# Expert stage: indices, gates and destinations read in place, and the first four experts' weights loaded one stage earlier

## The chip, the cores and the metric

The kernel runs on one core of one Trainium2 chip. The metric is the device time of a whole execution in microseconds (us), the median of several runs. A second source is one profiled execution, in which the hardware profiler records each instruction and each DMA transfer. Engine names are those of the profile: PE is the matrix engine (TensorE), PEld its weight load, DVE is VectorE, ACT is ScalarE, POOL is GpSimd and SP is SyncE, which here only issues transfers (SPq is its queue of instructions).

## The reference

One layer of a streaming encoder: attention and an RWKV-7 recurrence from one projection, a LayerNorm, then a mixture of experts with two levels of routing, and a second LayerNorm. The part that matters here is the mixture of experts:

```
def hier_moe(h, moe_w):                      # h: 2048 + 32 tokens x 1024
    grp  = argmax(h @ w_gr + b_gr)           # one of 4 groups
    e_in = (h @ w_er + b_er)[grp]            # 8 experts of that group
    top_p, top_i = top_k(softmax(e_in), 2)   # two experts for each token
    gate = top_p / sum(top_p) * p_grp
    ...                                      # assignments sorted by expert, in blocks of rows
    def run_block(xb, e):
        return (silu(xb @ w_eg[e]) * (xb @ w_eu[e])) @ w_ed[e]
    y = zeros.at[token].add(run_block(...) * gate)
```

There are 32 experts, each with three matrices of 1024 x 256 (or 256 x 1024) floats, 1024 KB each. All data is float32.

## The kernel before

The program is a sequence of stages, each a block in which every engine runs its own list of instructions, with a barrier between two stages: mixer, attention, router, dispatch, experts, combine. All loops are written out, so the order on each engine is fixed when the program is built.

**Dispatch** (from line 1903) sorts the assignments. It fills 64 blocks of 128 rows (`NBLK`); each expert's rows begin at a new block, and the blocks left over at the end repeat the last expert with rows that go to a spare place. It leaves three tables in SBUF: `kept_tokens` (the output row of every block row, an integer), the gates in the first 64 columns of `kept_onehot`, and in the next 256 columns the row numbers that the gathers use, as floats (lines 2062 to 2069). SP does nothing in this stage.

**Experts** (from line 2072) runs over the 64 blocks, two to a turn, with two copies (s = 0 and 1) of every buffer. For one block:

- POOL gathers the block's 128 rows of `scr_hx` with four indirect DMAs (line 2153) into `ex_x`; the row numbers are first copied to a small buffer `ex_idx` (line 2149).
- DVE transposes them in four pieces to `ex_xT` (line 2321).
- PE multiplies by the gate and the up matrix (line 2252, 16 matmul records each), ACT takes the tanh (2200), DVE makes `ex_hid` (2328, 2332), PE transposes that (2267), ACT copies it to `ex_hT` (2205), PE multiplies by the down matrix (2276, 8 records).
- ACT writes `ex_y` from `ex_down`, scaled by the row's gate, in two halves (line 2212). The gate column is a copy that POOL made in `ex_gcol` (line 2160).
- POOL adds `ex_y` into `scr_acc` in HBM with one indirect DMA that accumulates (line 2171); the row numbers are a copy in `ex_dest` (line 2168). Two additions may not be under way at once, since two blocks can name the same row, so each waits for the one before it to have landed.

Within a turn i POOL's order is: both gate copies, the eight gathers of turn i + 2, then the addition of block 0, then that of block 1 (`turn`, line 2174). ACT's order is fixed too: for each block the tanh, the copy to `ex_hT` of the block before, and the result of the block before. ACT does not wait for the landed addition itself before it writes `ex_y` again; it waits for POOL's marks `gate0` and `dest0` (line 2210), which stand behind such a wait on POOL.

The weights lie in four slots (`SLOTS`). SP loads expert e into slot e mod 4 when expert e - 4 has left it (line 2127) and when expert e - 2 has landed (line 2124), so at most two loads are under way. PE may start an expert when `ready` says that its weights are there.

The lines quoted in the prediction are in the functions below.

Of the kernel before, what the change touches and what calls it, by code (L numbers as in the profile page):

```python
# [142 lines left out]
    ).split(),  # L143
    "gather_gpsimd": (
        "idx0 idx1 "
    ).split(),
    "add_gpsimd": (
        "gate0 gate1 dest0 dest1 "
# [193 lines left out]
def first_of_router(nc):  # L342
# [5 lines left out]
    return t  # L348

# [1286 lines left out]
def router(nc, io, scr, keep):  # L1636
# [6 lines left out]
    with ExitStack() as ctx:  # L1643
# [12 lines left out]
        ahead = scr["first_of_dispatch"] = Placed(nc, given.start - 4 * (3 * P + 96 + 56), cst=[3, P], nums=[96], cols=[56])  # L1656
# [246 lines left out]
def dispatch(nc, io, scr, keep):  # L1903
# [3 lines left out]
    with ExitStack() as ctx:  # L1907
# [12 lines left out]
        given = scr["first_of_dispatch"]  # L1920
        cst, nums = given.tiles["cst"], given.tiles["nums"][:, 0:KB + NBLK]
# [35 lines left out]
        block = ctx.enter_context(nc.Block())  # L1957

# [113 lines left out]
def experts(nc, io, scr, keep):  # L2072
# [4 lines left out]
    with ExitStack() as ctx:  # L2077
        def sb(name, shape, dt=F32):
# [6 lines left out]
        nought = sb("nought", [P, 1])  # L2085
        spare = [sb(f"spare{s}", [P, 1]) for s in range(2)]
        spare_y = [sb(f"spare_y{s}", [P, 1]) for s in range(2)]
        dest = [sb(f"dest{s}", [P, 1], I32) for s in range(2)]
        gcol = [sb(f"gcol{s}", [P, 1]) for s in range(2)]
        started = ctx.enter_context(nc.semaphore("ex_started"))  # L2090
        wg, wu, wd = sb("wg", [P, SLOTS, KC * FE]), sb("wu", [P, SLOTS, KC * FE]), sb("wd", [P, SLOTS, FC * D])

        idx, x, xT, th, hid, hT, y = ([sb(f"{n}{s}", shape, dt) for s in range(2)] for n, shape, dt in (
            ("idx", [P, 4], I32), ("x", [P, 4, FE], F32), ("xT", [P, KC, P], F32), ("th", [P, FE], F32),
# [6 lines left out]
        apol, bpol = Steps(nc, ctx, "gather_gpsimd"), Steps(nc, ctx, "add_gpsimd")  # L2101
        w_in = [Dmas(nc, ctx, f"ex_w_in{s}", 3, 1) for s in range(SLOTS)]
# [7 lines left out]
        def _(sp):  # L2110
            sp.dma_start(ident[:], io["ident"]).then_inc(const.sem, 16)
            for s in range(SLOTS):
                sp.sem_inc(w_in[s].sem, 16 * 3)

            def turn(t):
# [6 lines left out]
                for s, e in enumerate(es):  # L2122
# [4 lines left out]
                    sp.wait_ge(down.sem, free_at[s])  # L2127
                    for dst, src in ((wg, io["w_eg"]), (wu, io["w_eu"])):
                        w_in[s].go(sp.dma_start(dst[:, s, :], src[e].rearrange("a (p k) n -> (a p) (k n)", k=KC)))
# [6 lines left out]

        @block.gpsimd
        def _(g):
            g.memset(nought[:], 0.0).then_inc(started, 1)
            g.wait_ge(started, 1)  # L2140

            for own in (apol, bpol):
                g.sem_inc(own.sem, own.per)
# [474 lines left out]
```

## Time and profile before

| | us |
|---|---|
| median of 3 runs | 3268.62 (3267.7 to 3272.02) |
| the profiled execution, whole | 3262.0 |
| its span (first to last instruction) | 3259.1 |
| PE busy (matmul) | 2919.8 (90%) |
| DVE, ACT, POOL busy | 1740.4, 967.0, 587.6 |
| DMA engines, mean | 95 GB/s, 310.23 MB |
| mean granted PE clock | 0.954 |

The times in the rows below are microseconds from the start of the span, so that stages can be placed: dispatch begins at 2416, experts at 2452.7, combine at 3201.5. "Idle before" is the time an engine stood still before an instruction, with what ended it.

### The profile page before, as it was taken

The page shows a single profiled execution, that of the slowest core. Times are in us where ns is not written, and L with a number is a line of the kernel's source. Part 1 is how long each engine was busy: PE and PEld are TensorE (multiplying, and loading weights), DVE is VectorE, ACT ScalarE, POOL GpSimd, SP SyncE. Part 2 cuts the span into 40 slices and gives each one's busy share as a digit, 9 for nine tenths or more (in the row PEclk, how much of TensorE's full clock was granted, in tenths as well). Part 3 has the DMA queues.
Part 4 walks back from the last instruction along what each step waited for, and adds up shares of the span by engine and source line. Part 5 has one row for each costly group of instructions (what it writes and reads, how often), then busy time and mean ns, then how long its engine had stood idle before and what let it go on. Part 6 is the DMA issues. An engine that isn't in the chain of part 4 may idle for free. (4 is left out here: it accounts for less than half of the span.)

```text
span 3259.1 us, 66235 instructions
## 1 busy us (share of the span) xinstructions
PE 2919.8 (90%) x26600; PEld 2220.4 (68%) x26600; DVE 1740.4 (53%) x3820; ACT 967.0 (30%) x2497; POOL 587.6 (18%) x875
## 2 busy tenths in 40 slices
PE   7999999999999999669898998899957999989990
PEld 6888888888888888545555555555535776666770
DVE  1666666666666666558686868622253222222225
ACT  2333333333333333234443444312211111111115
POOL 0001000000000000010000000011104645555650
PEclk9999999999999999689999999999968999999995
DMA  6111121211111112420101010034318899776546
GB/s 192 35 38 36 37 40 37 39 37 36 37 37 36 38 37 40 93 86 1 38 1 39 1 35 1 34 117 129 129 52 304 257 371 291 241 228 164 104 95 245
DMA packets 337227, 310.23 MB, mean 95 GB/s; under 512 B 235201, under 2 KB 290529, under 8 KB 322529
## 3 DMA queue, kind: packets, MB, share of 16 engines
q1 hardware_dynamic: 315424, 238.88, 24.1%
q0 software_dynamic: 21504, 67.13, 9.2%
q8 instruction: 217, 3.56, 0.5%
q14 instruction: 82, 0.66, 0.1%
HBM read 208.12 MB, written 84.42 MB: 90 GB/s over the span
## 5 line engine op out<-in xcount | busy, mean ns | idle before, releaser
L802 PE MATMUL mx_bank<-mx_xT,mx_w_in 128*128 128x128 f32 x5168 | 647.6, 282 | 17.3 <-DVEq L286 13.8
L802 PEld LDWEIGHTS mx_bank<-mx_xT,mx_w_in 128*128 128x128 f32 x5168 | 606.3, 195 | 83.3 <-issue 60.6
L1485 PE MATMUL at_bank<-pl_kT,pl_qT 128*128 128x512 f32 (+5 forms) x656 | 291.1, 530 | 2.3 <-issue 2.3
L1457 ACT ACTIVATE at_PQ<-at_bank,at_nms 128x512 f32<-128x512 f32 (+5 forms) x328 | 192.7, 596 | 253.6 <-DVE at_nms L1585 252.1
L2276 PE MATMUL ex_down<-ex_wd,ex_hT 128*128 x512 | 236.4, 605 | 26.9 <-ACT ex_hT L2205 25.4
L2153 POOL DMA_INDIRECT ex_x<-scr_hx,ex_idx x256 | 247.0, 965 | 68.1 <-issue 60.1
L2252 PE MATMUL ex_gate<-ex_wg,ex_xT 128*128 x1024 | 234.1, 382 | 17.5 <-SPq L2125 17.5
L2252 PEld LDWEIGHTS ex_gate<-ex_wg,ex_xT 128*128 128x128 f32 x1024 | 196.3, 192 | 71.3 <-issue 47.3
L2212 ACT ACTIVATE ex_y<-ex_down,ex_gcol 128x512 f32<-128x512 f32 x128 | 81.0, 683 | 525.4 <-POOL ex_gcol L2160 186.1
L2252 PE MATMUL ex_up<-ex_wu,ex_xT 128*128 x1024 | 231.6, 379 | 0.0
L1628 DVE COPY at_PT<-at_bank 128x512 f32<-128x512 f32 (+3 forms) x328 | 196.3, 600 | 45.7 <-PE at_bank L1497 28.0
L1516 PEld LDWEIGHTS at_bank<-at_PT,at_vals 128*64 128x64 f32 (+1 forms) x2208 | 118.0, 137 | 150.4 <-issue 78.1
L2321 DVE STREAM_TRANSPOSE ex_xT<-ex_x 128x256 f32<-128x256 f32 x256 | 141.0, 608 | 145.3 <-DMA ex_x<-scr_hx,ex_idx 145.3
L1497 PE MATMUL at_bank<-pl_at_ident,at_PQ 128*128 128x128 f32 x1104 | 186.0, 284 | 22.9 <-ACT at_PQ L1457 12.8
L2252 PEld LDWEIGHTS ex_up<-ex_wu,ex_xT 128*128 128x128 f32 x1024 | 190.3, 191 | 23.2
L1497 PEld LDWEIGHTS at_bank<-pl_at_ident,at_PQ 128*128 128x128 f32 x1104 | 127.4, 142 | 107.6 <-issue 44.8
L1581 DVE TENSOR_REDUCE at_mx<-at_bank 128x1 f32<-128x512 f32 (+5 forms) x328 | 188.4, 574 | 15.9 <-PE at_bank L1485 10.5
L653 POOL TENSOR_TENSOR mx_AR<-mx_u,mx_ep 128x512 f32<-128x512 f32 x17 | 20.0, 1177 | 963.2 <-DVE mx_kh L1142 963.2
L1516 PE MATMUL at_bank<-at_PT,at_vals 128*64 128x128 f32 (+1 forms) x2208 | 166.5, 283 | 24.3 <-DVE at_o_sb L1603 24.2
L698 ACT ACTIVATE mx_pr<-mx_bank 128x256 f32<-128x256 f32 (+1 forms) x68 | 37.0, 544 | 509.1 <-PE mx_bank L802 499.5
L2276 PEld LDWEIGHTS ex_down<-ex_wd,ex_hT 128*128 128x128 f32 x512 | 97.1, 193 | 131.7 <-issue 129.4
L2328 DVE SCALAR_TENSOR_TENSOR ex_th<-ex_th,ex_gate 128x256 f32<-128x256 f32 x64 | 26.8, 419 | 264.1 <-ACT ex_th L2200 208.2
(315 smaller groups left out, 4681.3 us busy)
## 6 DMA issues: line engine op xcount, KB each, us to landing
ex_wg<-in_w_eg SPq DMA_DIRECT2D x32, 1024.0 KB
ex_wu<-in_w_eu SPq DMA_DIRECT2D x32, 1024.0 KB
ex_wd<-in_w_ed SPq DMA_DIRECT2D x32, 1024.0 KB
mx_x<-in_x SPq DMA_DIRECT2D x76, 128.0 KB, 3.8
pl_ro_x<-in_x SPq DMA_DIRECT2D x17, 512.0 KB, 4.3
scr_hx<-ro_h SPq DMA_DIRECT2D x17, 512.0 KB, 2.6
scr_acc<-ro_ha SPq DMA_DIRECT2D x17, 512.0 KB, 3.1
co_r<-scr_acc SPq DMA_DIRECT2D x17, 512.0 KB, 5.6
```

What stands on the lines that cost most here:

```text
L802: ins = pe.matmul(dst, w_in[:, k, col:col + n], xT[:, k, :], start=(k == 0), stop=(k == KC - 1))
L1457: ins = a.activation(PQ[:, n % NP, 0:full], b[:, 0:full], ACT.Exp, bias=bias, scale=SCALE, accum_out=sums[:, j, h, 1 + gi:2 + gi])
L1485: t.mark(pe.matmul(bank[n % SB][:, 0:wd], qT[h][keys(h), j * P:(j + 1) * P], kT[h][keys(h), k0 * P:k0 * P + wd], start=True, stop=True), f ...
L1497: ins = pe.transpose(bank[SB + n % TB][0:rows, c:c + P], PQ[:, n % NP, c:c + rows], ident[:, :])
L1516: ins = pe.matmul(bank[7][64 * h:64 * h + 64, 0:P], vals[0:rows, k0 + s, 64 * h:64 * h + 64], PT[0:rows, m % NPT, s, :], start=(gi == 0 an ...
L1581: t.do(v.tensor_reduce(mx[:, 1 + gi:2 + gi], b[:, 0:wd], AX.X, ALU.max), f"max{n}")
L1628: ins = v.tensor_copy(PT[:, n % NPT, 0:full, :], b[:, 0:full * P].rearrange("p (a n) -> p a n", a=full))
L2153: x_in[s].go(g.indirect_dma_start(x[s][:, k, :], None, rows, bass.IndirectOffsetOnAxis(ap=idx[s][:, k:k + 1], axis=0)))
L2212: ins = a.activation(y[s][:, 512 * n:512 * n + 512], down_b[n][:, :], ACT.Copy, scale=gcol[s][:, 0:1])
L2252: ins = pe.matmul(b[s][:, 0:FE], xT[s][:, k, :], wv[:, k * FE:(k + 1) * FE], start=(k == 0), stop=(k == KC - 1))
L2276: ins = pe.matmul(down_b[n][:, :], hT[s][:, m, :], wv[:, m * D + n * 512:m * D + (n + 1) * 512], start=(m == 0), stop=(m == FC - 1))
L2321: ins = v.transpose(xT[s][:, :, 32 * h:32 * h + 32], x[s][:, h, :].rearrange("p (i k) -> p k i", k=KC))
```

## The change

Four things are changed, all in the last part of the program.

1. The copies on POOL go. One cast on DVE at the start of the experts stage makes all 256 row numbers integers (`ex_idx`, 128 x 256), and the gathers read their column there. The additions read their column of `kept_tokens`, and ACT reads its gate column of `kept_onehot`. The tiny additions of zeros (`ex_spare`, `ex_spare_y`) that stood ahead of POOL's DMAs go as well.
2. ACT's write of `ex_y` waits for the landing of that buffer's own addition one turn before, and for no mark of POOL.
3. POOL's order becomes: addition of block 0, four gathers for block 0 of turn i + 2, addition of block 1, four gathers for block 1.
4. The weight slots are given a fixed place at the top of SBUF, and SP loads the first four experts in the dispatch stage, with no wait among them. The constants of dispatch move down to make room.

```
@@ first_of_experts, load_expert (new), used by dispatch and experts
+def first_of_experts(nc):
+    t = Placed(nc, top_of_weights(nc), wg=[SLOTS, KC * FE], wu=[SLOTS, KC * FE], wd=[SLOTS, FE // P * D])
+    t.w_in = [Dmas(nc, None, f"ex_w_in{s}", 3, 1) for s in range(SLOTS)]
+    return t
+
+def load_expert(sp, io, t, s, e):
+    wg, wu, wd = (t.tiles[n] for n in ("wg", "wu", "wd"))
+    for dst, src, k in ((wg, io["w_eg"], KC), (wu, io["w_eu"], KC), (wd, io["w_ed"], FE // P)):
+        t.w_in[s].go(sp.dma_start(dst[:, s, :], src[e].rearrange("a (p k) n -> (a p) (k n)", k=k)))
@@ dispatch
+        @block.sync
+        def _(sp):
+            for s in range(SLOTS):
+                sp.sem_inc(weights.w_in[s].sem, 16 * weights.w_in[s].n)
+                load_expert(sp, io, weights, s, bass.ds(s, 1))
@@ experts, SP
-                    sp.wait_ge(down.sem, free_at[s])
-                    for dst, src in ((wg, io["w_eg"]), (wu, io["w_eu"])):
-                        w_in[s].go(sp.dma_start(dst[:, s, :], ...))
-                    w_in[s].go(sp.dma_start(wd[:, s, :], ...))
+                    if t.i > 0:
+                        sp.wait_ge(down.sem, free_at[s])
+                        load_expert(sp, io, given, s, e)
@@ experts, POOL
+            g.wait_ge(listed, 1)
+            def gathers(i, s):
+                Turn(g, None, i).w0(xt, f"xT{s}")
+                for k in range(4):
+                    at = 4 * (2 * i + s) + k
+                    x_in[s].go(g.indirect_dma_start(x[s][:, k, :], None, rows,
+                                                    bass.IndirectOffsetOnAxis(ap=idx[:, at:at + 1], axis=0)))
+            def add(i, s):
+                if s == 1:
+                    g.wait_ge(y_add[0].sem, y_add[0].done(i))
+                elif i > 0:
+                    g.wait_ge(y_add[1].sem, y_add[1].done(i - 1))
+                Turn(g, None, i).w(bact, f"y{s}")
+                ...
+            for i in range(turns):
+                for s in range(2):
+                    add(i, s)
+                    if i < turns - 2:
+                        gathers(i + 2, s)
@@ experts, ACT
-                t.w(bpol, ("gate0", "dest0")[s])
+                if t.i > 0:
+                    t.left(y_add[s])
+                at = 2 * t.i + s
                 for n in range(2):
-                    ins = a.activation(y[s][...], down_b[n][:, :], ACT.Copy, scale=gcol[s][:, 0:1])
+                    ins = a.activation(y[s][...], down_b[n][:, :], ACT.Copy, scale=row_gate[:, at:at + 1])
@@ experts, DVE
+            v.tensor_copy(idx[:], keep["onehot"][:, NBLK:5 * NBLK]).then_inc(listed, 1)
```

How the order moves is seen in one turn on POOL, in the middle of the experts stage. First before; the names behind "waits" are semaphores: `down_scalar` counts ACT's results, `turned_vector` DVE's transposes, `ex_y_add0` and `ex_y_add1` the landed additions.

```order
L2160 COPY ex_gcol0<-kept_onehot 128x1 [waits down_scalar]
L2160 COPY ex_gcol1<-kept_onehot 128x1 [waits down_scalar]
L2149 CAST ex_idx0<-kept_onehot 128x4 [waits turned_vector]
L2151 TENSOR_TENSOR ex_spare0<-ex_nought 128x1 [waits gather_gpsimd]
L2153 DMA ex_x0<-scr_hx,ex_idx0 128x256 x4
L2149 CAST ex_idx1<-kept_onehot 128x4 [waits turned_vector]
L2151 TENSOR_TENSOR ex_spare1<-ex_nought 128x1 [waits gather_gpsimd]
L2153 DMA ex_x1<-scr_hx,ex_idx1 128x256 x4
L2168 COPY ex_dest0<-kept_tokens 128x1 [waits ex_y_add1]
L2170 TENSOR_TENSOR ex_spare_y0<-ex_nought 128x1 [waits down_scalar,add_gpsimd]
L2171 DMA scr_acc<-ex_y0,ex_dest0 2304x1024
L2168 COPY ex_dest1<-kept_tokens 128x1 [waits ex_y_add0]
```

The same turn on POOL in the changed kernel, up to the next turn's first addition:

```order
L2169 DMA scr_acc<-ex_y0,kept_tokens 2304x1024 [waits down_scalar,ex_y_add1]
L2158 DMA ex_x0<-scr_hx,ex_idx 128x256 [waits turned_vector]
L2158 DMA ex_x0<-scr_hx,ex_idx 128x256 x3
L2169 DMA scr_acc<-ex_y1,kept_tokens 2304x1024 [waits down_scalar,ex_y_add0]
L2158 DMA ex_x1<-scr_hx,ex_idx 128x256 [waits turned_vector]
```

Eight gathers stood between two additions at one place and none at the other; now four stand between any two, and nothing but DMAs is left on POOL.

On ACT, one step of the pipeline before (tanh of block 1, then `ex_hT` and result of block 0):

```order
L2200 ACTIVATE ex_th1<-ex_gate1 128x256 [waits expert_vector,expert_tensor]
L2205 ACTIVATE ex_hT0<-ex_turn0 128x256 [waits down_tensor,turn_tensor]
L2212 ACTIVATE ex_y0<-ex_down0,ex_gcol0 128x512 [waits add_gpsimd,down_tensor]
L2212 ACTIVATE ex_y0<-ex_down1,ex_gcol0 128x512
L2200 ACTIVATE ex_th0<-ex_gate0 128x256 [waits expert_vector,expert_tensor]
```

and now:

```order
L2188 ACTIVATE ex_th1<-ex_gate1 128x256 [waits expert_vector,expert_tensor]
L2193 ACTIVATE ex_hT0<-ex_turn0 128x256 [waits down_tensor,turn_tensor]
L2201 ACTIVATE ex_y0<-ex_down0,kept_onehot 128x512 [waits ex_y_add0,down_tensor]
L2201 ACTIVATE ex_y0<-ex_down1,kept_onehot 128x512
L2188 ACTIVATE ex_th0<-ex_gate0 128x256 [waits expert_vector,expert_tensor]
```

The order is the same; only the semaphore ahead of `ex_y` is another one.

## Rows read from the trace of the kernel before

**Rows 1.** Windows (columns: busy us of each engine, PE clock, DMA share, GB/s)
```profile
2609.00:2629.00 20.00, 20.00 (x80) 14.66 (x80) 5.92 (x12) 3.84 (x8) 12.56 (x20) 1.00 1.02 365
...
2669.00:2689.00 20.00, 17.67 (x76) 13.79 (x74) 5.16 (x10) 1.97 (x5) 7.54 (x13) 1.00 1.02 383
2689.00:2709.00 20.00, 18.16 (x57) 11.73 (x58) 6.09 (x12) 3.58 (x8) 10.32 (x14) 0.83 0.96 323
...
3049.00:3069.00 20.00, 20.00 (x80) 14.69 (x79) 6.01 (x12) 3.85 (x8) 12.72 (x20) 1.00 0.52 103
```

**Rows 2.** Timeline of PE: down products (start, us, what, idle before)
```profile
2665.36 3.60 PE L2276 MATMUL ex_down<-ex_wd,ex_hT 128*128 x8
2675.94 3.60 PE L2276 MATMUL ex_down<-ex_wd,ex_hT 128*128 x8
2690.84 6.25 PE L2276 MATMUL ex_down<-ex_wd,ex_hT 128*128 x8 [4.17 <-ACT ex_hT L2205]
...
2985.45 3.69 PE L2276 MATMUL ex_down<-ex_wd,ex_hT 128*128 x8 [0.19 <-issue]
```

**Rows 3.** Waits in the experts stage: total us, times, longest
```profile
POOL ex_dest L2168 <- DMA scr_acc<-ex_y,ex_dest: 217.2, 33, 10.9
...
ACT ex_y L2212 <- POOL ex_gcol L2160: 186.1, 19, 13.7
```

**Rows 4.** Timeline of all engines around the first stall
```profile
2662.86 1.04 POOL L2153 DMA_INDIRECT ex_x<-scr_hx,ex_idx  x1 [0.15 <-issue]
...
2666.73 0.97 POOL L2153 DMA_INDIRECT ex_x<-scr_hx,ex_idx  x1 [0.30 <-issue]
...
2673.66 1.64 POOL L2171 DMA_INDIRECT scr_acc<-ex_y,ex_dest  x1
...
2676.40 2.21 DVE L2321 STREAM_TRANSPOSE ex_xT<-ex_x 128x256 f32<-128x256 f32 x4 [10.36 <-DMA ex_x<-scr_hx,ex_idx]
...
2679.37 3.62 PE L2252 MATMUL ex_gate<-ex_wg,ex_xT 128*128 x16
...
2681.27 2.23 DVE L2321 STREAM_TRANSPOSE ex_xT<-ex_x 128x256 f32<-128x256 f32 x4 [1.90 <-DMA ex_x<-scr_hx,ex_idx]
...
2686.20 0.18 POOL L2168 COPY ex_dest<-kept_tokens 128x1 int32<-128x1 int32 x1 [10.89 <-DMA scr_acc<-ex_y,ex_dest]
...
2688.84 1.26 ACT L2212 ACTIVATE ex_y<-ex_down,ex_gcol 128x512 f32<-128x512 f32 x2 [13.70 <-POOL ex_gcol L2160]
```

**Rows 5.** Timeline of SP: last of three issues of one weight load
```profile
2680.43 0.47 SPq L2130 DMA_DIRECT2D ex_wd<-in_w_ed  x1
```

**Rows 6.** Timeline around the start of dispatch and of the experts
```profile
2415.99 1.16 DVE L2001 TENSOR_TENSOR di_both<-kept_onehot 128x544 f32<-128x544 f32 x1 [0.54 <-PEq L1643]
...
2451.52 0.67 DVE L2068 TENSOR_SCALAR kept_onehot<-di_spread,di_group 128x256 f32<-128x256 f32 x1 [0.77 <-PE di_spread L1982]
2452.68 0.10 POOL L2139 MEMSET ex_nought<- 128x1 f32 x1 [36.11 <-POOLq L1907]
...
2457.86 0.95 POOL L2153 DMA_INDIRECT ex_x<-scr_hx,ex_idx  x1 [0.30 <-issue]
...
2464.92 2.18 DVE L2321 STREAM_TRANSPOSE ex_xT<-ex_x 128x256 f32<-128x256 f32 x4 [12.73 <-DMA ex_x<-scr_hx,ex_idx]
...
2468.83 0.33 SPq L2129 DMA_DIRECT2D ex_wg<-in_w_eg  x1
...
2468.91 6.29 PE L2252 MATMUL ex_gate<-ex_wg,ex_xT 128*128 x16 [17.51 <-SPq L2125]
```

**Rows 7.** DMA issues: median us from issue to landing
```profile
pl_w_o<-in_w_o SPq DMA_DIRECT2D x1, 4096.0 KB, 12.1
```

**Rows 8.** Timeline of the last blocks
```profile
3181.54 1.58 POOL L2171 DMA_INDIRECT scr_acc<-ex_y,ex_dest  x1 [0.44 <-issue]
...
3187.85 0.18 POOL L2168 COPY ex_dest<-kept_tokens 128x1 int32<-128x1 int32 x1 [4.74 <-DMA scr_acc<-ex_y,ex_dest]
...
3188.57 1.57 POOL L2171 DMA_INDIRECT scr_acc<-ex_y,ex_dest  x1 [0.27 <-issue]
```

More of the change, by code:

```diff
@@ L142 @@
         "h_T0 y0 h_T1 y1 "
[L143 to L148, printed above, removed]
     ).split(),
@@ L2084, in experts @@
         ident = sb("ident", [P, P])
[L2085 to L2094, printed above, removed]
+        row_gate, tokens = keep["onehot"], keep["tokens"]
+        idx = sb("idx", [P, 4 * NBLK], I32)
+        listed = ctx.enter_context(nc.semaphore("ex_listed"))
+        given = scr["first_of_experts"]
+        wg, wu, wd = (given.tiles[n] for n in ("wg", "wu", "wd"))
+        x, xT, th, hid, hT, y = ([sb(f"{n}{s}", shape, dt) for s in range(2)] for n, shape, dt in (
+            ("x", [P, 4, FE], F32), ("xT", [P, KC, P], F32), ("th", [P, FE], F32),
             ("hid", [P, FE], F32), ("hT", [P, FC, P], F32), ("y", [P, D], F32)))
@@ L2138, in _ @@
         def _(g):
[L2139 to L2143, printed above, removed]
+            g.wait_ge(listed, 1)
             rows = scr["hx"].rearrange("t (a n) -> (t a) n", a=4)
-            def gathers(t):
-                for s in range(2):
-                    t.w0(xt, f"xT{s}")
-                    t.do(g.tensor_copy(idx[s][:], keep["onehot"][:, bass.ds(t.i * 8 + (NBLK + 4 * s), 4)]), f"idx{s}")
-                    g.tensor_tensor(spare[s][:], nought[:], nought[:], ALU.add)
-                    for k in range(4):
-                        x_in[s].go(g.indirect_dma_start(x[s][:, k, :], None, rows,
-                                                        bass.IndirectOffsetOnAxis(ap=idx[s][:, k:k + 1], axis=0)))
@@ L2174, in turn @@
-            def turn(i, more):
-                t = Turn(g, bpol, i)
-                gates(t)
-                if more:
-                    gathers(Turn(g, apol, i + 2))
-                    apol.whole()
-                for s in range(2):
-                    add(t, s)
-                bpol.whole()
-            for i in range(2):
-                gathers(Turn(g, apol, i))
-                apol.whole()
-            turn(0, True)
-            for i in range(1, turns - 2):
-                turn(i, True)
@@ L2190, in _ @@
-            for i in range(turns - 2, turns):
-                turn(i, False)
+            def gathers(i, s):
[10 more added lines that the diff above has]
+                Turn(g, None, i).w(bact, f"y{s}")
+                at = 2 * i + s
+                y_add[s].go(g.indirect_dma_start(scr["acc"], bass.IndirectOffsetOnAxis(ap=tokens[:, at:at + 1], axis=0),
+                                                 y[s][:], None, compute_op=ALU.add))
@@ L2192, in _ @@
+            for i in range(2):
+                for s in range(2):
+                    gathers(i, s)
+            for i in range(turns):
+                for s in range(2):
+                    add(i, s)
+                    if i < turns - 2:
+                        gathers(i + 2, s)
             for s in range(2):
```

27 lines of the change are left out of this document (6 added, 21 removed).

## The prediction

> **What bounds the kernel now.** I first read the table of windows over the experts stage, since the change is there. It shows PE busy all 20.00 us of most stretches, also while the DMA share is 1.02, and short of that from 2669 on; in 2689 to 2709 the granted clock is 0.83 instead of 1.00 [rows 1]. So PE sets the pace except in a middle part. The timeline of PE's down products gives the sizes. Undisturbed, one block follows another after 2675.94 - 2665.36 = 10.58 us (10.573 over many). From 2675.94 to 2985.45 there are 26 blocks in 309.5 us [rows 2]; at 10.573 they would take 274.9. **34.6 us are lost there**, the slow clock after the long stop (6.25 us for a product that takes 3.60) among them. After 2985 no block is late: all 32 experts have been loaded, and the DMA share is 0.52 [rows 1].
>
> Next the list of waits: ACT's write of ex_y waited 186.1 us for POOL's gate copy, and POOL 217.2 us for additions to land [rows 3]. The timeline of the first stall shows how they hang together [rows 4]. POOL issues eight gathers (the first at 2662.86), and only then the addition (2673.66), whose y had long been written. The addition lands at 2686.20, behind the gathers, which had landed at 2676.40 and 2681.27. ACT may write ex_y at 2688.84, after 13.70 us; its next two instructions wait behind it, and PE with them. POOL's cycle is thus gathers (11 us) plus an addition to its landing (12.5 us at the stall) plus the second addition and the copies: longer than two blocks of PE (21.1 us) whenever the landing is slow.
>
> **Part 1: copies gone, order turned, ACT's own wait.** An addition is now issued when its y is there and the one before it has landed. On POOL a block costs one addition of 1.64 us and four gathers at about 1.25 us (2662.86 to 2667.70 for four), 6.8 us of 10.57 [rows 4], so POOL is not the limit by its issues. ACT waits for an addition issued a whole turn, 21.1 us, earlier; 12.5 us, the longest landing that I found, is well inside that, and had eight gathers ahead of it, where now there are four. So ACT's wait goes. What is late next is either x or the weights.
>
> *x.* The four gathers now stand behind the addition. When must x be there? A gate product starts 3.43 us after a down product (2679.37 after 2675.94 [rows 2, 4]), and the one that reads this x comes two blocks later, so 24.6 us after the start of the down product D whose block is added just ahead of the gathers. Four transposes take 2.2 us, so they must start by D + 22.4. The y is ready at about D + 5.1 (3.6 for the product, 1.26 for ACT, 0.2 between), the addition and the four gathers are issued 1.6 + 5.2 us later, at D + 11.9. That leaves 10.5 us from the last gather's end to its landing. In the most crowded place the last gather of the first four ended at 2667.70 and x was there at 2676.40: 8.7 us [rows 4]. It fits by 1.8 us. This bound is narrow; if the addition ahead makes landings 3 us longer, about ten crowded blocks lose 1 us each.
>
> *Weights.* Crowded, one block of an expert that has only one moves 3.15 MB of weights and 1.05 MB of gather and addition. At the 365 to 383 GB/s of the full stretches [rows 1] that is 11.3 us, 0.7 more than PE's 10.57. The load at 2680.43 was issued as soon as the down product from 2675.94 was through [rows 2, 5], so SP was not waiting for a landing then. Since no load is issued before the last but one has landed, and that one was issued two blocks earlier, a load took at most 21.1 us, and PE wants it three blocks (31.7 us) after its issue. The lead of 10.5 us covers 15 such blocks at 0.7 us; the full stretch from 2609 to 2709 is 9 or 10 blocks long. I take 3 us of the 34.6 as staying: nothing if the lead holds, 12 if both x and weights run short (7 of weights and 5 of x). **-31.6 us** (-34.6 to -22).
>
> A rule bears on the crowded part. Three portions of 512 KB (four gathers, four gathers, one addition) landed at 2676.40, 2681.27 and 2686.20, 4.9 us each, with the weight loads beside them [rows 4]: 9.8 us for a block, under 10.57. The Trainium skill ("DMA: Bandwidth & Descriptors", queues, rings and completion order) says that a DMA engine takes queue rows in turn, a packet at a time, so the POOL queue should get about half of the engines when SP's is full. Alone, a block's gathers and addition take 0.52 x 10.57 = 5.5 us of all engines [rows 1], so by that rule 11.0 us in a crowd, 0.4 more than PE: over ten blocks 4 us, within the slack of 21.1 - 12.5 = 8.6 us of ACT's wait. The sum is the same by either.
>
> **Part 2: four experts' weights in dispatch.** Before, SP could let PE start only at 2468.83, when the first expert had landed, and PE started at 2468.91; x was transposed at 2464.92 + 2.18 = 2467.1 [rows 6]. Now 12 MB are issued from 2416. By the load of 4096 KB in 12.1 us [rows 7] they take about 36 us and are there at 2452 to 2453, with the stage's end at 2452.7, and only the first three MB are needed at once. So the chain is x alone. The cast of 128x256 on DVE costs at most the 0.67 us of the last op of dispatch on as many elements, I take 0.4; with the semaphore the first gather starts at about 2453.6, where POOL's own memset, cast and zero-add had put it at about 2453.9 (the fourth started at 2457.86, at 1.25 us each). The fourth ends at 2458.6 (2458.81 before). Before, landing took another 6.1 us, with two weight loads running beside it [rows 6]. Without them I take 2 us, as POOL's own list of four is spread over 5 us and an idle queue has only the last 128 KB left; the bounds are 0 and 6.1. Transposed at 2460.6 + 2.2 = 2462.8, PE starts at 2462.9: **-6.0 us** (-1.8 to -8). The first 16 products run at the low clock before (6.29 us) and will again.
>
> By the same page's fit for one transfer (anatomy of one DMA: 2.0 us plus the bytes at 436 GB/s) the last gather would land 2.3 us after its issue, 1.35 after its end, and part 2 would be -6.6. For an addition of 512 KB it would give 3.2 us, where the trace has 6.3 (3181.54 to 3187.85 [rows 8]), so I don't use it.
>
> The twelve issues, about 0.4 us each, lie on SP, which is idle in dispatch; nothing waits behind them. Whether 12 MB of landing weights slow the small DVE operations of dispatch no row shows directly: I take 0, at most 4 us.
>
> **Part 3: the end.** The last addition was issued at 3188.57, 0.72 us after the one before it had landed, with a copy and a zero-add in between [rows 8]. Now about 0.3 us after; the one before it goes out some 0.4 us sooner. **-0.8 us** (0 to -1.2). Combine is untouched.
>
> **Sum**: -31.6 - 6.0 - 0.8 = -38.4 us. Against the profiled execution's 3262.0 that is 3223.6. The median of the runs is 6.6 us above the profiled one; I carry that over: **3230.2 us**.
>
> **Rivals.**
>
> *A. The crowd is the new bound.* With POOL's cycle gone, PE waits for x or `ready` between 2620 and 2770. For it: DMA share 1.02 and 11.3 us against 10.57. Against: PE ran full through 2609 to 2669 at that share, and the weights taken out of the start are not part of this stretch. Price: the 12 us of the upper bound instead of 3: 3239. Should the loss go on into the two-block experts, up to 20 us: 3247.
>
> *B. The start is not won.* PE still starts about 2467, because the gathers' landing has a floor of its own near the 6.1 us seen, or dispatch grows by the 4 us. For it: an addition takes 6.3 us to land in the empty late part. Against: an addition moves all its 512 KB after its issue. Price: +4: 3234.
>
> *C. Slower: additions in a chain.* Every addition still waits for the landing of the one before, and now four gathers precede each one, so there is no more an addition that follows another directly. If each takes the 12.5 us of the worst landing and 0.3 to issue, the period is 12.8 us for the 45 blocks up to 2985 (19 before 2676, 26 after): 45 x 2.2 = 99 us instead of 34.6, and with parts 2 and 3: 3269 + 64 - 7 = 3326. It decides from a mean of (34.6 + 6.8) / 45 + 10.57 = 11.5 us per addition on. Against: the 12.5 us had eight gathers in front of it, and three portions needed 4.9 us each [rows 4].
>
> *D. ACT's wait was not PE's.* If PE's stalls come from the DMA in any case, removing POOL's marks wins only the 2.6 us from the landing at 2686.20 to 2688.84 [rows 4] in each of about 13 stalled turns; that alone would still be 34 us. So this gives nearly the forecast and I don't hold it apart.
>
> **How the numbers follow.** Forecast 0.66, A 0.20, B 0.09, C 0.05. The lowest time is all bounds at their best, 3268.6 - 34.6 - 8 - 1.2 = 3225, less 2 for the scatter of runs; the upper end takes in A to 3247. Range 3222 to 3248. A measurement tells about 0.2% (6.5 us) from no change. Forecast, A and B are all faster: 0.95. Between them and C: same 0.02, slower 0.03.
>
> **What would show it.** Right: down products 10.57 us apart also between 2676 and 2985 of the old time, PE clock 1.00 throughout, ACT's ex_y waiting for PE only; first gate product about 10 us after the stage's start instead of 16.2; DMA share near 1 in dispatch and DVE's operations there as long as before. A would show as DVE waiting for ex_x, or PE for SP's `ready`, in the crowded part; B as a late first transpose; C as POOL waiting over 10 us for ex_y_add in most turns, with ACT behind it. I am wrong if the period stays above 10.9 us in the middle part.

## The result, and the profile after

The changed kernel takes 3219.57 us (median of 4 runs, 3218.14 to 3224.67), the one before 3270.32 (median of 4, 3267.7 to 3272.5). The ratio is 0.9848, 95% interval 0.9831 to 0.9865: 1.5% faster. The forecast was 3230.2, in a range from 3222 to 3248, so the time lies 2.4 us below the low end. The profiled execution after is 3219.8 whole; against the 3262.0 of before it is 42.2 us shorter, where the sum of the prediction said 38.4.

First the windows over the experts stage, in the columns of [rows 1]; the first two lie in dispatch.

```profile
2409.00:2429.00 20.00, 4.45 (x8) 2.28 (x8) 13.87 (x44) 0.22 (x1) 0.61 (x1) 0.50 0.73 292
2429.00:2449.00 20.00, 12.23 (x78) 11.54 (x78) 17.50 (x37) 0.00 (x0) 0.00 (x0) 0.70 0.81 337
...
2609.00:2629.00 20.00, 20.00 (x80) 14.70 (x79) 5.87 (x12) 3.24 (x8) 10.88 (x10) 1.00 1.03 379
...
2669.00:2689.00 20.00, 19.49 (x79) 14.30 (x78) 5.85 (x12) 3.85 (x8) 10.02 (x10) 1.00 1.03 368
2689.00:2709.00 20.00, 19.01 (x75) 13.51 (x74) 5.85 (x12) 3.25 (x7) 9.78 (x10) 1.00 1.03 369
...
3049.00:3069.00 20.00, 20.00 (x80) 14.70 (x79) 5.73 (x12) 3.64 (x8) 9.92 (x9) 1.00 0.45 102
```

Where PE was busy 17.67 and 18.16 us of 20 and the clock once fell to 0.83 [rows 1], it is now busy 19.49 and 19.01 at a clock of 1.00. It is not quite 20.00, so a little is still lost there. The DMA share of 0.73 and 0.81 in dispatch is the early weights: 292 and 337 GB/s over 20 us each.

The waits of the experts stage (columns as in [rows 3]):

```profile
ACT ex_y L2201 <- PE ex_down L2265: 410.6, 64, 6.5
...
DVE ex_xT L2310 <- DMA ex_x<-scr_hx,ex_idx: 329.6, 62, 11.0
...
POOL scr_acc L2169 <- DMA scr_acc<-ex_y,kept_tokens: 122.5, 27, 5.4
...
PE ex_gate L2241 <- DVE ex_xT L2310: 11.5, 1, 11.5
```

ACT's result waits for PE alone, 64 times out of 64 blocks; the 186.1 us behind POOL's gate copy are gone. POOL's wait for landings went from 217.2 to 122.5 us, its longest from 10.9 to 5.4. PE waited for x once for 11.5 us, which is the start of the stage. One wait grew: DVE's for the gathered x is now 329.6 us over 62 blocks, where before it was 145.3 us over 33 (the row below). It mostly costs nothing, but it says that x now comes with little to spare.

```profile
DVE ex_xT L2321 <- DMA ex_x<-scr_hx,ex_idx: 145.3, 33, 12.7
```

The start, in the timeline (columns as in [rows 6]):

```profile
2413.52 1.16 DVE L2019 TENSOR_TENSOR di_both<-kept_onehot 128x544 f32<-128x544 f32 x1 [0.54 <-PEq L1654]
...
2450.26 0.29 DVE L2329 CAST ex_idx<-kept_onehot 128x256 int32<-128x256 f32 x1 [0.53 <-PEq L1918]
2451.28 1.17 POOL L2158 DMA_INDIRECT ex_x<-scr_hx,ex_idx  x1 [37.18 <-DVE ex_idx L2329]
...
2455.27 0.95 POOL L2158 DMA_INDIRECT ex_x<-scr_hx,ex_idx  x1 [0.30 <-issue]
2458.01 2.18 DVE L2310 STREAM_TRANSPOSE ex_xT<-ex_x 128x256 f32<-128x256 f32 x4 [7.46 <-DMA ex_x<-scr_hx,ex_idx]
...
2460.47 5.85 PE L2241 MATMUL ex_gate<-pl_wg,ex_xT 128*128 x16 [11.52 <-DVE ex_xT L2310]
```

From the first instruction of dispatch to the first gate product it is 2460.47 - 2413.52 = 46.95 us; before, 2468.91 - 2415.99 = 52.92 [rows 6]. The fourth gather's end at 2456.22 and its landing at 2458.01 are 1.8 us apart.

The table below gathers the same differences for each profiled execution, in us. "Dispatch begins" is the start of its first DVE operation; "start" goes from there to the first gate product; "PE" from the start of the first gate product to that of the last down product, and "stalls" is how much longer the down products took, from the first to the last, than one block each 10.573 (the last follows after 5.36 in before and after alike); "rest" is the time from the last down product's start to the end of the whole, combine and what lies around the span included. The last column is the range of all timed runs. The profiled execution is one of them, except in the first line: the 3262.0 us of before is not among its four.

| kernel | profiled | dispatch begins | start | PE | stalls | rest | all runs |
|---|---|---|---|---|---|---|---|
| before | 3262.0 | 2416.0 | 52.9 | 712.3 | 34.7 | 80.8 | 3267.7 to 3272.5 |
| after | 3219.8 | 2413.5 | 46.9 | 680.3 | 3.2 | 79.0 | 3218.1 to 3224.7 |
| before_again | 3270.1 | 2419.3 | 52.8 | 718.3 | 40.6 | 79.6 | 3259.7 to 3274.0 |
| weights_only | 3253.8 | 2411.9 | 47.1 | 716.4 | 39.5 | 78.4 | 3253.8 to 3266.6 |
| pool_act_only | 3224.6 | 2411.8 | 52.4 | 680.5 | 2.6 | 79.9 | 3222.9 to 3224.6 |
| old_order | 3236.2 | 2418.1 | 46.9 | 692.4 | 15.1 | 78.8 | 3234.3 to 3236.2 |
| new_order_copies | 3232.2 | 2414.6 | 53.0 | 684.5 | 7.2 | 80.1 | 3232.2 to 3235.0 |
| act_wait_only | 3237.7 | 2411.6 | 52.8 | 694.1 | 16.9 | 79.2 | 3237.7 to 3259.0 |
| light_weights | 3226.0 | 2417.0 | 52.9 | 677.4 | 0.0 | 78.8 | 3225.3 to 3227.1 |
| gathers_first | 3221.0 | 2418.3 | 46.9 | 676.9 | 0 | 78.8 | 3218.6 to 3222.9 |
| after_again | 3213.5 | 2407.5 | 46.9 | 680.1 | 2.9 | 79.1 | 3206.5 to 3219.8 |
| gathers_first_idx | 3209.9 | 2408.7 | 46.6 | 677.1 | 0 | 77.6 | 3209.9 to 3216.9 |

In the first two lines the 42.2 us are: 2.5 before dispatch, where the instructions are the same, 6.0 in the start, 32.0 on PE (31.5 of them stalls), and 1.8 in the rest, of which 0.5 lies in the last blocks, 0.3 in combine and 0.9 outside the span (rounded, each for itself).

### The profile page after: what moved, and what is told of

It reads as the page before. It is cut to its first block and busy times, and to the rows that moved or that the text cites. A ratio compares the mean times of both kernels' runs of the same rounds, so it can differ in the third digit from the quotient of the medians.

```text
span 3217.8 us, 65907 instructions
## 1 busy us (share of the span) xinstructions
PE 2905.5 (90%) x26600; PEld 2216.2 (69%) x26600; DVE 1740.2 (54%) x3821; ACT 970.5 (30%) x2497; POOL 529.4 (16%) x554
## 5 line engine op out<-in xcount | busy, mean ns | idle before, releaser
L2310 DVE STREAM_TRANSPOSE ex_xT<-ex_x 128x256 f32<-128x256 f32 x256 | 141.6, 611 | 329.6 <-DMA ex_x<-scr_hx,ex_idx 329.6
L2241 PE MATMUL ex_gate<-pl_wg,ex_xT 128*128 x1024 | 234.2, 382 | 13.7 <-DVE ex_xT L2310 11.5
L2241 PEld LDWEIGHTS ex_gate<-pl_wg,ex_xT 128*128 128x128 f32 x1024 | 195.8, 192 | 68.7 <-issue 45.0
L2265 PE MATMUL ex_down<-pl_wd,ex_hT 128*128 x512 | 230.3, 593 | 1.5 <-ACT ex_hT L2193 1.5
L2241 PE MATMUL ex_up<-pl_wu,ex_xT 128*128 x1024 | 231.6, 380 | 0.0
L2241 PEld LDWEIGHTS ex_up<-pl_wu,ex_xT 128*128 128x128 f32 x1024 | 190.4, 191 | 22.9
L2201 ACT ACTIVATE ex_y<-ex_down,kept_onehot 128x512 f32<-128x512 f32 x128 | 81.0, 684 | 410.6 <-PE ex_down L2265 410.6
L2265 PEld LDWEIGHTS ex_down<-pl_wd,ex_hT 128*128 128x128 f32 x512 | 97.4, 190 | 96.6 <-issue 93.4
L2169 POOL DMA_INDIRECT scr_acc<-ex_y,kept_tokens x64 | 103.3, 1615 | 271.8 <-ACT ex_y L2201 130.9
```

The source lines that it names most:

```text
L2169: y_add[s].go(g.indirect_dma_start(scr["acc"], bass.IndirectOffsetOnAxis(ap=tokens[:, at:at + 1], axis=0), y[s][:], None, compute_op=ALU.add))
L2241: ins = pe.matmul(b[s][:, 0:FE], xT[s][:, k, :], wv[:, k * FE:(k + 1) * FE], start=(k == 0), stop=(k == KC - 1))
L2265: ins = pe.matmul(down_b[n][:, :], hT[s][:, m, :], wv[:, m * D + n * 512:m * D + (n + 1) * 512], start=(m == 0), stop=(m == FC - 1))
L2310: ins = v.transpose(xT[s][:, :, 32 * h:32 * h + 32], x[s][:, h, :].rearrange("p (i k) -> p k i", k=KC))
```

## The experiments

The short names are those of the table. Ratios are to the kernel before, run on the same chip; where the changed kernel is the base of an edit, that is said. Three chips were used: one for the first four of these experiments, one for the next four (new_order_copies, act_wait_only, light_weights and gathers_first), one for the last two. Rows of the table that come from different chips are compared from dispatch on, not as a whole.

**The kernel before, unchanged**: is the difference between its profiled execution and its median a constant?

> The kernel before, unchanged, for a second profiled execution. Theory V (variance in the stalls): the step that failed is the carry-over of 6.6 us from the profiled execution to the median; most executions of the kernel before lose more than 34.6 us between the down products, because POOL's cycle reacts to how weight loads and gathers fall together. Then an execution near 3270 us shows 40 to 46 us of stalls there, and one near 3262 shows 34 to 36. Rival O (other stages): the stalls are 34 to 36 us whatever the time, and the difference of 6 to 10 us lies before dispatch, or around the span. Median expected 3268 to 3272 either way.

Its median was 3268.3 us, its ten runs went from 3259.74 to 3274.01, ratio 1.0006 (0.9995 to 1.0017). The profiled execution took 3270.1 and had 40.6 us of stalls instead of 34.7. Dispatch began 3.3 us later too. The median is at the low end of what was expected, the stalls are those of theory V, and part of rival O holds as well. Waits of ACT, and PE's down products (columns as in [rows 2, 3]):

```profile
ACT ex_y L2212 <- POOL ex_gcol L2160: 229.4, 23, 12.6
ACT ex_y L2212 <- POOL ex_dest L2168: 208.8, 23, 9.5
```

```profile
2594.65 3.60 PE L2276 MATMUL ex_down<-ex_wd,ex_hT 128*128 x8
2606.84 3.70 PE L2276 MATMUL ex_down<-ex_wd,ex_hT 128*128 x8 [1.45 <-ACT ex_hT L2205]
...
2640.58 3.70 PE L2276 MATMUL ex_down<-ex_wd,ex_hT 128*128 x8 [0.18 <-ACT ex_hT L2205]
2653.83 5.39 PE L2276 MATMUL ex_down<-ex_wd,ex_hT 128*128 x8 [2.41 <-ACT ex_hT L2205]
...
2702.72 5.39 PE L2276 MATMUL ex_down<-ex_wd,ex_hT 128*128 x8 [2.71 <-ACT ex_hT L2205]
```

The wait for the gate copy is 229.4 us where it was 186.1 [rows 3]. PE's first late down product is at 2606.84, 84 us earlier than the first of [rows 2], and behind the longer stops (2.41 and 2.71 us) the product is slow: 5.39 us instead of 3.60. So the stalls are a length of time that varies between executions of one kernel, here by 5.9 us, and of the two executions the profiled 3262.0 had fewer.

**Only the early weights** (the kernel before, with the slots' fixed place in SBUF, dispatch's SP block and no load in the first turn).

```
+        @block.sync                    # in dispatch
+        def _(sp): ... load_expert(sp, io, weights, s, bass.ds(s, 1))
+                    if t.i > 0:        # in experts
                         sp.wait_ge(down.sem, free_at[s])
```

> The kernel before with only the early loads of the first four experts. Theory S: gains 2 to 6 us (PE starts when x is there, 10 to 12 us after the stage's start), stalls in the middle as before: 3264 to 3268. Rival I: the earlier start moves POOL's cycle against the weight loads and the stalls grow or shrink by more than 5 us: below 3260 or above 3270.

The start came down from 52.8 to 47.1 us and the stalls stayed, 39.5. The runs have a median of 3260.95 us, ratio 0.9986 (0.9974 to 0.9998); the range that I had given, 3264 to 3268, missed it by 3 us. The runs are 5.2 us below the 3266.17 of before beside them, about the 5.7 of the start; my range rested on the first median, with too little allowed for the spread.

```profile
ACT ex_y L2233 <- POOL ex_gcol L2181: 218.9, 22, 12.4
...
PE ex_gate L2273 <- DVE ex_xT L2342: 11.7, 1, 11.7
```

PE's one long wait at the start is now for x and not for the weights, as part 2 had it, and ACT's wait for POOL is untouched by it.

**All but the early weights** (the changed kernel, loads in experts as before).

```
-        @block.sync                    # in dispatch
+                    sp.wait_ge(down.sem, free_at[s])      # in experts, for every turn
+                    load_expert(sp, io, given, s, e)
```

> The changed kernel with the weights of the first four experts loaded in the experts stage again, so that only the changes on POOL, ACT and DVE are left. Theory S (sum of parts): stalls between down products 3 to 5 us, PE starts about 16 us after the experts stage begins, so 6 us slower than the changed kernel: 3225 to 3228. Rival I (the parts depend on one another): without the early loads the run of one-block experts comes with a shorter lead or the first blocks are late, and it loses 10 us or more against the changed kernel: above 3230.

Median 3223.68 us, ratio 0.987 (0.9853 to 0.9886), 1.3 us below the range expected. Stalls 2.6, start 52.4.

```profile
ACT ex_y L2196 <- PE ex_down L2260: 410.6, 64, 6.5
...
PE ex_gate L2236 <- SPq L2133: 17.0, 1, 17.0
```

The start waits 17.0 us for SP's `ready` as before, and ACT's waits are those of the changed kernel to the digit. So the two halves of the change don't touch each other: one takes the stalls, one takes 6 us of the start.

**POOL's old order** (the changed kernel, with both groups of gathers ahead of both additions).

```
                 for s in range(2):
-                    add(i, s)
                     if i < turns - 2:
                         gathers(i + 2, s)
+                for s in range(2):
+                    add(i, s)
```

> The changed kernel with POOL's old order: eight gathers of turn i + 2, then both additions; copies and marks stay out, ACT waits for its own buffer's addition, weights early. Theory C (POOL's cycle is the limit): the cycle of gathers (10.0 us), addition to its landing (9 to 12.5 us) and second addition (1.6 us) is still over 21.1 us in the crowded part, but shorter by about 2 to 3 us a turn, and ACT may run ahead by it; stalls 5 to 15 us instead of 3.4, median 3222 to 3232. Rival D (marks alone): as the prediction's D has it, taking away POOL's marks is enough, and it equals the changed kernel within 3 us.

Median 3235.12 us, ratio 0.9905 (0.9888 to 0.9921); stalls 15.1. Both lie just above what theory C gave (3232 and 15), and far from rival D. ACT's own wait is in place here, and it is not short:

```profile
ACT ex_y L2202 <- DMA scr_acc<-ex_y,kept_tokens: 273.4, 31, 12.8
...
POOL scr_acc L2169 <- DMA scr_acc<-ex_y,kept_tokens: 215.7, 29, 12.6
```

```profile
2650.29 1.62 POOL L2169 DMA_INDIRECT scr_acc<-ex_y,kept_tokens  x1 [0.30 <-issue]
...
2662.65 1.27 ACT L2202 ACTIVATE ex_y<-ex_down,kept_onehot 128x512 f32<-128x512 f32 x2 [12.28 <-DMA scr_acc<-ex_y,kept_tokens]
...
2664.65 3.70 PE L2266 MATMUL ex_down<-pl_wd,ex_hT 128*128 x8 [1.86 <-ACT ex_hT L2194]
```

The addition went out at 2650.29, behind its eight gathers, and landed 12.3 us later; ACT sat 12.28 us in front of it and PE lost 1.86.

**The new order alone** (the kernel before, with copies, marks and zero-adds, an addition ahead of each four gathers).

```
                 gates(t)
-                if more:
-                    gathers(Turn(g, apol, i + 2))
-                    apol.whole()
                 for s in range(2):
                     add(t, s)
+                    if more:
+                        gathers(Turn(g, apol, i + 2), (s,))
...
```

> The kernel before with only POOL's order turned (addition 0, four gathers, addition 1, four gathers); copies, POOL's marks and ACT's wait for them stay, weights as before. Theory C (the cycle of gathers and landing is the cause): the order alone takes the eight gathers out of the landing, and an addition is issued a block earlier, so ACT is held up little although it still waits for POOL's marks: stalls 3 to 12 us instead of 35 to 41, median 3230 to 3238. Rival M (the marks are the cause, since old order without them already lost only 15 us): the marks now stand behind four gathers and a landing, and the stalls stay above 20 us: median above 3248.

Median 3234.74 us, ratio 0.991 (0.9889 to 0.9931); stalls 7.2, and the start as before, 53.0.

```profile
ACT ex_y L2213 <- PE ex_down L2277: 339.9, 53, 6.5
ACT ex_y L2213 <- POOL ex_gcol L2160: 82.0, 11, 8.7
...
POOL ex_dest L2168 <- DMA scr_acc<-ex_y,ex_dest: 116.0, 31, 4.7
```

POOL's wait for landings is at once that of the changed kernel (116.0 us, 122.5 there), and in only 11 blocks does ACT still wait for a gate copy. So theory C's 3 to 12 us hold and rival M, stalls above 20, does not. The copies, with ACT's wait for POOL's marks, cost 7.2 - 2.6 = 4.6 us of stalls against the kernel without early weights.

**ACT's wait alone** (the kernel before without the gate copies, its POOL order kept).

```
-                t.w(bpol, ("gate0", "dest0")[s])
+                if t.i > 0:
+                    t.left(y_add[s])
...
-                ... scale=gcol[s][:, 0:1]
+                ... scale=keep["onehot"][:, at:at + 1]
```

> The kernel before with only ACT's wait changed: it waits for its own buffer's landed addition and reads the gate column in place; the gate copies go, the index and destination copies, the zero-adds and POOL's old order stay, weights as before. Rival M, and the prediction's D: most of the gain comes from this, stalls 15 to 20 us, as in the old order without copies (15.2). Theory C: POOL's cycle is longer here than without copies by about 2 us a turn, so stalls of 20 to 30 us; median 3245 to 3258.

Median 3246.97 us, ratio 0.9949 (0.9935 to 0.9963); stalls 16.9 in the profiled execution, and runs up to 3259.0, the widest spread of all. The profiled execution, 3237.7, is the fastest of the ten, 9.2 us below the median, so 16.9 is likely the low end of this kernel's stalls. By the stalls rival M was expected (15 to 20), by the median theory C (3245 to 3258); the run doesn't choose between them.

```profile
ACT ex_y L2207 <- DMA scr_acc<-ex_y,ex_dest: 293.1, 33, 13.2
```

The mark is gone and the wait is not: 33 times it ends with the addition's landing, up to 13.2 us. This is rival D, and it is refuted as I had priced it: with the wait for POOL's marks removed 17 us of stalls or more stay, and the medians differ by 3265.3 - 3246.97 = 18.3 us, not by the 34 that I had given it.

**Half of the later weight bytes left out** (the kernel before; from the fifth expert on only 512 of 2048 columns of the up and the down matrix are loaded, so 1.5 of 3 MB of each expert are left out, and its outputs are not the layer's).

```
+                    part = 2048 if t.i == 0 else 512
+                    for dst, src, n in ((wg, io["w_eg"], 2048), (wu, io["w_eu"], part)):
+                        w_in[s].go(sp.dma_start(dst[:, s, 0:n], ...))
+                    w_in[s].go(sp.dma_start(wd[:, s, 0:part], ...))
```

> The kernel before, but from the fifth expert on only a quarter of the up and of the down matrix is loaded (1.5 MB less of 3 MB for each of 28 experts is moved); all instructions on POOL, ACT, DVE and PE are as before. Theory C: POOL's cycle is over two blocks of PE only when landings are slow, and they are slow from the weight loads beside them; with half the bytes an addition lands in 6 to 9 us and the stalls fall from 35 to 41 us to under 10: median 3232 to 3242. Rival Q (POOL's own queue is the cause: eight gathers ahead of the addition, whatever lies beside): stalls stay above 25 us, median above 3252.

Stalls 0.0; median 3225.87 us, ratio 0.9883 (0.9862 to 0.9904). That is 6 us below the range expected, since not under 10 us of stalls but none were left.

```profile
2669.00:2689.00 20.00, 20.00 (x83) 15.16 (x82) 4.86 (x11) 3.85 (x8) 12.71 (x20) 1.00 0.88 252
```

```profile
2664.37 1.64 POOL L2174 DMA_INDIRECT scr_acc<-ex_y,ex_dest  x1
...
2671.67 0.18 POOL L2171 COPY ex_dest<-kept_tokens 128x1 int32<-128x1 int32 x1 [5.66 <-DMA scr_acc<-ex_y,ex_dest]
```

With POOL's order and copies all as before, an addition behind eight gathers lands in 7.3 us instead of 12.5 [rows 4], and nothing is late; rival Q, POOL's queue by itself, is refuted. With new_order_copies beside it, most of the stalls need both: a POOL cycle in which everything stands in a row, and weight loads beside it that stretch the landings.

**Gathers ahead of the addition, block by block** (the changed kernel), for the 3 us that are left.

```
                 for s in range(2):
-                    add(i, s)
                     if i < turns - 2:
                         gathers(i + 2, s)
+                    add(i, s)
```

The crowded stretch of the changed kernel, which this edit aims at:

```profile
2624.71 3.60 PE L2265 MATMUL ex_down<-pl_wd,ex_hT 128*128 x8
...
2628.34 1.27 ACT L2201 ACTIVATE ex_y<-ex_down,kept_onehot 128x512 f32<-128x512 f32 x2 [6.46 <-PE ex_down L2265]
...
2632.18 1.62 POOL L2169 DMA_INDIRECT scr_acc<-ex_y,kept_tokens  x1 [4.15 <-DMA scr_acc<-ex_y,kept_tokens]
...
2637.90 0.95 POOL L2158 DMA_INDIRECT ex_x<-scr_hx,ex_idx  x1 [0.30 <-issue]
...
2643.43 1.62 POOL L2169 DMA_INDIRECT scr_acc<-ex_y,kept_tokens  x1 [4.58 <-ACT ex_hT L2193]
...
2647.86 2.20 DVE L2310 STREAM_TRANSPOSE ex_xT<-ex_x 128x256 f32<-128x256 f32 x4 [8.60 <-DMA ex_x<-scr_hx,ex_idx]
...
2650.32 3.72 PE L2241 MATMUL ex_gate<-pl_wg,ex_xT 128*128 x16 [0.73 <-issue]
...
2653.91 1.61 POOL L2169 DMA_INDIRECT scr_acc<-ex_y,kept_tokens  x1 [3.82 <-DMA scr_acc<-ex_y,kept_tokens]
...
2697.32 1.61 POOL L2169 DMA_INDIRECT scr_acc<-ex_y,kept_tokens  x1 [4.14 <-DMA scr_acc<-ex_y,kept_tokens]
```

The gate product starts 0.26 us after the transpose's end, so x is what came last, and the additions are issued as each predecessor lands: five periods from 2643.43 to 2697.32, 10.78 us each against PE's 10.57. The gathers stand behind them and slip with them, about 0.2 us a block. One of them can be followed: the y of the block whose down product starts at 2624.71 is written at 2629.61, but its addition goes out only at 2632.18, when the one before has landed; the last of the four gathers behind it ends at 2638.85, and its x is there 9.0 us later, at 2647.86.

> The changed kernel with the four gathers of block s issued ahead of the addition of block s instead of behind it. In the changed kernel 3.2 us are lost in the crowded stretch, where DVE starts its transposes late. Theory X: the gathers there wait behind an addition that itself waits up to 4 us for the landing of the one before; issued first they land about 5 us earlier, POOL has time for them before y is written, and the loss goes to 0 to 1 us: 1 to 3 us less than the changed kernel, 3216 to 3219. Rival B (bandwidth): 11.3 us of bytes against 10.57 us of work sets the loss, whatever the order: 3 us stay, 3218 to 3222, or more if the additions now land later and hold up ACT.

Stalls 0, 3.2 to 3.4 us of PE's stretch gained. The median is 3220.08 us, ratio to before 0.9865 (0.9844 to 0.9887), in the runs no different from the changed kernel. So the profile bears theory X out, and the median does not: it lies above the 3216 to 3219 of theory X and inside the rival's 3218 to 3222.

```profile
DVE ex_xT L2310 <- DMA ex_x<-scr_hx,ex_idx: 21.6, 12, 7.4
```

DVE's wait for x fell from 329.6 us to 21.6: x is now there before it is wanted. The additions are no faster for it:

```profile
2614.60 1.62 POOL L2169 DMA_INDIRECT scr_acc<-ex_y,kept_tokens  x1 [4.49 <-DMA scr_acc<-ex_y,kept_tokens]
...
2713.39 1.62 POOL L2169 DMA_INDIRECT scr_acc<-ex_y,kept_tokens  x1 [5.04 <-DMA scr_acc<-ex_y,kept_tokens]
```

These are nine periods of 10.98 us. With the same bytes the loss is gone, although the transfers still fall behind PE by 0.4 us a block in this stretch: the order decides whether x is behind them.

**The changed kernel, unchanged**: do its runs scatter less, with the stalls gone?

> The changed kernel, unchanged, for a second profile and more times. Theory V: the kernel before varies because its stalls do (34.7 us in one execution, 40.6 in another, 3258 to 3274 in all), and the changed kernel has next to none, so its executions lie closer together, 3216 to 3225, with stalls of 2 to 5 us in the profile; what is left of the variation is where dispatch begins (2411 to 2419). Rival: the changed kernel varies as much as before, over 10 us.

Median 3213.53 us, runs from 3206.46 to 3219.78, ratio 0.986 (0.9838 to 0.9882). My expectation of 3216 to 3225 for its runs failed. Stalls (2.9) and start (46.9) repeat; from dispatch's start to the end it took 806.1 us, and 806.3 the first time. Dispatch began 6.1 us earlier, at 2407.46 instead of 2413.52, and that is nearly the whole difference of 6.3. The kernel before was faster beside it as well, 3259.02 in the median. That the runs would scatter less without stalls is not borne out: 13.3 us over five runs here, 14.3 over ten for before_again.

**The same order, with the row numbers written as integers by dispatch** (the kernel with gathers first, without the cast).

```
-            do(v.tensor_scalar(oh[:, NBLK:5 * NBLK].rearrange("p (b g) -> p g b", g=4), ...
+            do(v.tensor_scalar(keep["idx"][:].rearrange("p (b g) -> p g b", g=4), ...
...
-            g.wait_ge(listed, 1)
-            v.tensor_copy(idx[:], keep["onehot"][:, NBLK:5 * NBLK]).then_inc(listed, 1)
```

> Gathers ahead of the addition, and the row numbers written as integers by the last operation of dispatch, so that POOL's first gather waits for no cast on DVE. The first gather starts 0.3 us after the stage begins instead of 1.07, PE 0.8 us earlier; stalls 0 as with gathers first (-3 us against the changed kernel). Together 3 to 4 us less than the changed kernel in the part from dispatch to the last block; median 3215 to 3218 if the earlier stages take the same time. Rival B: nothing measurable, within 1 us of the changed kernel, because the additions then land late.

Median 3213.37 us, ratio 0.9866 (0.9847 to 0.9885). The start is 46.6 us, 0.3 less, where I had expected 0.8. From dispatch on it is the shortest of all, 801.3 us against 806.1 to 806.3 of the changed kernel; 1.4 to 1.5 us of that lie behind the last down product, where nothing was changed. In the medians on one chip (3213.37 and 3213.53) there is no difference that these runs can tell.

## Why the prediction missed the time, step by step

**Part 1 holds.** Stalls of 34.6 us were to become 3, and 31.5 of 34.7 went. The mechanism was POOL's cycle, as read from [rows 4]. What the runs add is how it divides. The new order alone leaves 7.2, ACT's wait alone 16.9, and both together, without any copies, 2.6 to 3.2. ACT's wait without the copies but in the old order leaves 15.1. What the other copies are worth there isn't settled: 1.8 us by these two profiles, but about 7 by the medians (gains of 31.1 us, 5.7 of it from the start, and of 18.3), and the intervals of the two ratios are about 5 us each way. Each cuts the same cycle, so their gains don't add up: before's 34.7 to 40.6 less 7.2 is 28 to 33 us for the order, and less 16.9 is 18 to 24 for the wait.

**The 3 us that stay** were sized right, and by the form of rival A that has x late: the margin of 1.8 us at x was the narrow one, and no row shows PE waiting for `ready` in the crowd. But the margin did not go where the prediction looked for it, in slower landings. It gave a landing 8.7 us, and 9.0 were measured (2638.85 to 2647.86); it had the gathers issued by D + 11.9, and they were through at 2638.85 - 2624.71 = 14.1. The term that it put at nothing is the addition's own wait for the landing before it, 2632.18 - 2629.61 = 2.6 us.

The rule on queues taken in turn is one of the Trainium skill: it ("DMA: Bandwidth & Descriptors", queues, rings and completion order) has each DMA engine go round the queue rows that have work for it, a packet at a time. With half of the engines for POOL's queue the prediction had 11.0 us for a block's gathers and addition beside weight loads, and three portions of 4.9 us had given it 9.8; the changed kernel's additions have a period of 10.8, and 10.98 with the gathers first. The trace is in line with the rule but does not show it. The bytes alone give nearly the same, 4.2 MB at the 368 to 379 GB/s of the windows above or 11.1 to 11.4 us, and with the late share of the changed kernel's own window, 0.45 instead of 0.52, the rule would give 9.5. What is shown is that the 9.8 was too low, and that the effect came at the gathers behind the chain, not at ACT's slack.

**Part 2 holds**, -6.0 us for -6.0. Landing took 1.8 us after the last gather's end, where I took 2. Dispatch did not grow under the 292 and 337 GB/s: from its first operation to the cast it is 2450.26 - 2413.52 = 36.7 us, as before from 2415.99 to 2452.68 [rows 6]. Rival B is refuted by that and by the start of 46.9 us.

**Part 3**: -0.8 said, -0.5 measured. The last additions, with nothing else moving:

```profile
3141.08 1.55 POOL L2169 DMA_INDIRECT scr_acc<-ex_y,kept_tokens  x1 [8.96 <-ACT ex_hT L2193]
...
3147.44 1.55 POOL L2169 DMA_INDIRECT scr_acc<-ex_y,kept_tokens  x1 [4.81 <-DMA scr_acc<-ex_y,kept_tokens]
```

From one issue to the next it is 6.36 us, with no copy in between any more; before it was 7.03 [rows 8].

**Rival C** is refuted: even in the crowded stretch the additions follow each other every 10.8 us, not every 12.8. **Rival D** was no twin of the forecast: 17 us of stalls or more would have stayed.

**The step that failed is the last one of the sum: "The median of the runs is 6.6 us above the profiled one; I carry that over".** It treats the difference as a part of the kernel that the change doesn't touch. The runs show two parts instead. One is the stalls themselves, 34.7 us in one profiled execution and 40.6 in another; a change that removes the stalls removes the longer ones, too. The other is the stages before dispatch, which begin it anywhere from 2407.5 to 2419.3 us in kernels that do the same up to there. In the changed kernel nothing of the 6.6 is left: its median is 0.2 us below its profiled execution. Of the miss, 3230.2 - 3219.6 = 10.6 us, that makes 6.8; the other 3.8 lie between the two profiled executions. So the gain between medians is 45.5 and 50.8 us (3259.02 - 3213.53, 3270.32 - 3219.57), and between the two profiles 42.2, of which 39.7 lie from dispatch on. The profiled 3219.8 of after is 3.8 below my 3223.6, 2.5 of it in earlier stages and 0.9 around the span. These two are luck of the executions that were profiled, not an effect that any run shows.

The low end of the range failed with it. "All bounds at their best" gave 3225 from the median with the stalls of the profile; with 40.6 us of stalls instead of 34.6 in that execution it would have been 3219, less 2. How much of the 6.6 us was stalls and how much earlier stages in the first runs of before can't be said, since only one of them has a profile. In the profiled 3262.0 dispatch began at 2416.0, later than in seven of the other eleven executions of the table, so it was hardly the earlier stages that made it short. Between before and before_again it was 6.0 on PE (5.9 of them stalls) and 3.3 of earlier stages, less 1.2 elsewhere. And the changed kernel still scatters by 13.3 us, so where one execution lies against the median is in part chance, with or without stalls: act_wait_only's lay 9.2 below.

## What to carry to other kernels

When a change removes stalls, don't take their length from one profiled execution as if it were that of the median: here they were 34.7 and 40.6 us in two executions of one kernel, and that spread belongs to the gain and to the range. In a queue where each item waits for the landing of the one before, put what others wait for ahead of the link of the chain, not behind it (329.6 us of DVE's waits became 21.6, the last 3 us of stalls 0, though the medians can't tell so small a gain). Two fixes of one cycle are not added; each is priced against what the other leaves (alone they leave 16.9 and 7.2 of 35 to 41 us, together about 3).

## What the runs showed of the hardware

- An indirect addition of 512 KB into HBM lands 6.3 us after its issue with the DMA engines otherwise nearly idle (3141.08 to 3147.44), 7.3 us behind eight gathers with half the weight bytes left out, and 12.3 to 12.5 us behind eight gathers with full weight loads beside it. With the addition and its gathers the same, the weight loads beside them make the difference between hidden and late.
- 12 MB of weight loads at 292 to 337 GB/s beside a stage of small DVE and PE operations cost that stage nothing that can be seen (36.7 us both times).
- Stages with identical instructions end up to 11.8 us apart in different executions (dispatch begins at 2407.5 to 2419.3), while from there to the end the changed kernel repeats to 0.2 us in its two profiled executions. Nearly all of it arises in the first stage: attention's first operation starts at 1394.8 to 1407.4, and from there to dispatch it is 1011.4 to 1013.8 us in all twelve. The two lowest are the two on the third chip, but on the first chip alone it is still 2411.8 to 2419.3. What in that stage varies was not looked for.
